# Whole-expert weight loads in the middle of a mixture-of-experts stream

## The reference, cut to what matters

```
h = rms_norm(x, moe_norm)
logits = h @ router_w + router_b                  # 32 experts, top 4 of each token
for each expert e, for its tokens xb:
    gu = xb @ w_up[e] + b_up[e]                   # w_up[e]: 1024 x 2048 float32 = 8 MB
    x_glu, x_lin = split(gu, 2)                   # clamped at 7
    act = x_glu * sigmoid(1.702 * x_glu) * (x_lin + 1)
    y = act @ w_down[e] + b_down[e]               # w_down[e]: 1024 x 1024 float32 = 4 MB
x = x + sum over the token's experts of gate * y
```

## Time and profile before

| | |
|---|---|
| median of the runs | 1144.08 us |
| the profiled execution | 1143.59 us, its span 1141.8 us |
| PE busy | 1100.4 us (96%) |
| DVE, ACT, POOL busy | 334.5, 231.0, 20.9 us |
| read from HBM | 446.18 MB, 392 GB/s over the span |
| DMA share, from slice 9 on to the last but one | 9 tenths or more |

### The profile page before, as it was taken

The page is one execution under the profiler, slowest core; times in us unless marked ns, Lnnn a source line. Parts: engine busy times, 40 slices in busy tenths (PEclk is TensorE's granted clock), DMA queues, the critical chain, the costliest instruction groups (busy, mean ns, idle before and its releaser), DMA issues.

```text
span 1141.8 us, 14032 instructions
## 1 busy us (share of the span) xinstructions
PE 1100.4 (96%) x5777; PEld 528.3 (46%) x5777; DVE 334.5 (29%) x641; ACT 231.0 (20%) x331; POOL 20.9 (2%) x34
## 2 busy tenths in 40 slices
PE   8999999999999999999999999999999999999997
PEld 8999998433333333333333333333333333333336
DVE  6899997311111111111111111111111111111027
ACT  6555454210011010110100010100100000011026
POOL 1200000000000000000000000000000000000011
PEclk9999999999999999999999999999999999999999
DMA  9985589899999999999999999999999999999991
GB/s 301 351 298 158 184 314 385 345 429 432 429 429 430 432 432 432 429 430 430 430 428 432 432 432 432 430 430 425 431 429 436 430 432 432 424 426 429 428 396 52
DMA packets 41055, 447.75 MB, mean 392 GB/s; under 512 B 3459, under 2 KB 3707, under 8 KB 21851
## 3 DMA queue, kind: packets, MB, share of 16 engines
q1 hardware_dynamic: 39924, 444.43, 93.4%
q0 software_dynamic: 672, 1.99, 0.6%
q10 hardware_dynamic: 423, 0.82, 0.2%
HBM read 446.18 MB, written 1.05 MB: 392 GB/s over the span
## 4 chain that ended last, share of the span: by engine, by line
PE 68%; DMA 28%; DVE 1%; ACT 1%; issue 1%; SPq 0%; DVEq 0%; ACTq 0%
PE ps L2080 24%; PE ps L2120 15%; DMA down_ring<-in_expert_w_down_dram 15%; DMA up_ring<-in_expert_w_up_dram 12%; PE ps L1797 6%; PE ps L2134 4%; PE ps L1807 3%; PE ps L1984 3%; PE ps L1861 2%; PE ps L2238 2%; PE ps L1887 1%; ACT hT L995 1%; PE ps L1866 1%; PE ps L2108 1%; PE ps L2091 1%; PE ps L2101 1%
## 5 line engine op out<-in xcount | busy, mean ns | idle before, releaser
L2080 PE MATMUL ps<-up_ring,hT 128*64 128x512 f32 x1968 | 432.7, 597 | 8.9 <-DMA up_ring<-in_expert_w_up_dram 8.4
L2080 PEld LDWEIGHTS ps<-up_ring,hT 128*64 128x64 f32 x1968 | 143.7, 138 | 289.1 <-issue 274.9
L2120 PE MATMUL ps<-down_ring,hT 128*64 128x512 f32 x992 | 229.3, 605 | 18.6 <-DMA down_ring<-in_expert_w_down_dram 11.9
L1535 DVE TENSOR_SCALAR extra<-ps 128x512 f32<-128x512 f32 x32 | 22.1, 692 | 690.4 <-PE ps L2091 690.4
L2120 PEld LDWEIGHTS ps<-down_ring,hT 128*64 128x64 f32 x992 | 68.2, 138 | 155.1 <-issue 139.4
L990 ACT ACTIVATE work<-ps 128x512 f32<-128x512 f32 x31 | 18.5, 597 | 437.7 <-PE ps L2091 437.7
L2134 PE MATMUL ps<-hT,extra 64*128 64x512 f32 x256 | 72.0, 640 | 0.8 <-DVE hT L1575 0.8
L1797 PE MATMUL ps<-h_hi,w_hi 128*128 128x256 f32 x288 | 70.2, 284 | 0.0
L1797 PE MATMUL ps<-h_lo,w_hi 128*128 128x256 f32 x288 | 69.9, 283 | 0.0
L802 ACT ACTIVATE w_hi<-up_ring 128x2048 fp32r<-128x2048 f32 x28 | 53.5, 1915 | 60.7 <-DMA up_ring<-in_w_in_dram 25.7
L492 DVE TENSOR_TENSOR w_lo<-up_ring,w_hi 128x2048 fp32r<-128x2048 f32 x28 | 63.9, 2288 | 4.1 <-ACT w_hi L802 4.0
(11 more groups left out here) (317 smaller groups left out, 818.6 us busy)
## 6 DMA issues: line engine op xcount, KB each, us to landing
up_ring<-in_expert_w_up_dram SPq DMA_DIRECT2D x47, 4096.0 KB, 27.4
down_ring<-in_expert_w_down_dram SPq DMA_DIRECT2D x63, 2048.0 KB, 18.3
up_ring<-in_expert_w_up_dram SPq DMA_DIRECT2D x31, 2048.0 KB, 17.5
up_ring<-in_w_in_dram SPq DMA_DIRECT2D x21, 1024.0 KB, 7.4
up_ring<-in_branch_w_dram SPq DMA_DIRECT2D x6, 1024.0 KB, 5.0
up_ring<-in_w_out_dram SPq DMA_DIRECT2D x4, 1024.0 KB, 6.9
up_ring<-in_expert_w_up_dram SPq DMA_DIRECT2D x4, 1024.0 KB, 22.6
up_ring<-in_ple_gate_w_dram SPq DMA_DIRECT2D x4, 1024.0 KB, 25.9
```

Source lines behind the costliest of these rows:

```text
L1535: nc.vector.tensor_scalar(lin, ps[:, LIN, :], 1.0 + LIMIT, 1.0 - LIMIT, ALU.min, ALU.max).then_inc(lin_ready, 1)
L2080: ins = nc.tensor.matmul(ps[64 * g:64 * g + 64, GLU + side, :], xe_of(q, j)[:, k % 4, k // 4, :], gated_columns(w, side, g), start=(k == 0 ...
L2120: last = nc.tensor.matmul(ps[64 * g:64 * g + 64, Y, :], actT[:, r, c, :], down_units[:, c, D * r + 512 * g:D * r + 512 * (g + 1)], start=( ...
```

## The change

- `EARLY_LOADS` goes from 16 to 20, so the order turns at 20 to 25.
- `JOINED_DOWN` (experts 4 to 19): both down units in one load of 4 MB (`load_down_pair`), issued when the expert before has read both; PE waits for it once, ahead of the first unit.
- `WHOLE_UP` (experts 6 to 19): all four up units in one load of 8 MB (`load_up_all`, 64 KB in one piece per partition), issued when expert q - 2 has read all four; PE waits for it once, ahead of the first unit.
- Rows by eights: partition p holds rows 8p to 8p + 7 of `w_up`, for all experts and all kinds of load. The gather (`x_eights`, `x_pairs`) and `moe_gain` follow.
- PE's and ACT's loops: four rounds of the projection with two pairs of experts each (projection before experts 4, 8, 12, 16), and then a loop of its own over experts 20 to 27, whose loads come in halves again.
- Ahead of PE's loops stand two new waits, on the semaphores of the third up unit of each buffer, since within the loop the second half is not waited for.

```
-EARLY_LOADS = 16
+EARLY_LOADS = 20
 JOINED_UP = range(4, N_EXP - 4)
+JOINED_DOWN = range(JOINED_UP.start, EARLY_LOADS)
+WHOLE_UP = range(JOINED_UP.start + 2, EARLY_LOADS)
...
+            def load_up_all(j, e):
+                first = UP_UNITS * j
+                rows = expert_w_up[0, bass.ds(e, 1)].rearrange("a (p r) n -> p a (r n)", p=P)
+                sp.dma_start(up_units[:, first:first + UP_UNITS, :].rearrange("p s b -> p (s b)"), rows[:, 0, :]
+                             ).then_inc(up_loaded[first], 16)
...
+            def load_down_pair(e):
+                rows = expert_w_down[0, bass.ds(e, 1)].rearrange("a (p r) n -> p a (r n)", p=P)
+                sp.dma_start(down_ring[:, :, :].rearrange("p s b -> p (s b)"), rows[:, 0, :]
+                             ).then_inc(down_loaded[0], 16)
...
+            def refill_up_all(q, j, e):
+                sp.wait_ge(up_used, UP_UNITS * (q - 1))
+                load_up_all(j, e)
...
+            def refill_down_pair(q, e):
+                sp.wait_ge(down_used, DOWN_UNITS * (q - 1) + DOWN_UNITS)
+                load_down_pair(e)
...
             refill_up_pairs(e + 1, 1, e + 1)
-            refill_down(e, e)
+            refill_down_pair(e, e)
             with sp.Fori(e // 2 + 1, EARLY_LOADS // 2) as i:
                 for j in range(2):
-                    refill_up_pairs(2 * i + j, j, 2 * i + j)
-                    refill_down(2 * i + j - 1, 2 * i + j - 1)
+                    refill_up_all(2 * i + j, j, 2 * i + j)
+                    refill_down_pair(2 * i + j - 1, 2 * i + j - 1)
...
-                                                x_sb[:, a, 512 * g:512 * (g + 1)], start=(a == 0), stop=(a == TT - 1))
+                                                x_eights[:, a, g, :, :], start=(a == 0), stop=(a == TT - 1))
...
-                    elif c % 2 == 0:
-                        pe.wait_ge(up_loaded[UP_UNITS * j + c], 16 * turn + 16)
+                    elif c == 0:
+                        pe.wait_ge(up_loaded[UP_UNITS * j], 16 * turn + 16)
+                    elif c == 2 and (halves or isinstance(q, int)):
+                        before = 0 if isinstance(q, int) and q < WHOLE_UP.start else len(WHOLE_UP) // 2
+                        pe.wait_ge(up_loaded[UP_UNITS * j + c], 16 * (turn - before) + 16)
...
             pe.wait_ge(early_unit_loaded, 16)
+            for j in range(2):
+                pe.wait_ge(up_loaded[UP_UNITS * j + 2], 16 * WHOLE_UP.start // 2)
             with pe.Fori(0, PROJ_PARTS) as part:
...
+            with pe.Fori(EARLY_LOADS // 2, JOINED_UP.stop // 2) as i:
+                for j in range(2):
+                    expert(2 * i + j, j, i, part=PROJ_PARTS - 1, halves=True)
```

More of the change, by code:

```diff
@@ L104 @@
 FINAL_BANK = [4, 5, 6, 7, 0]
-EARLY_LOADS = 16
+EARLY_LOADS = 20
 JOINED_UP = range(4, N_EXP - 4)
+JOINED_DOWN = range(JOINED_UP.start, EARLY_LOADS)
+WHOLE_UP = range(JOINED_UP.start + 2, EARLY_LOADS)
 PROJ_PARTS = 4
-PAIRS = len(JOINED_UP) // 2 // PROJ_PARTS
-assert JOINED_UP.start + 2 * PAIRS * PROJ_PARTS == JOINED_UP.stop
+PAIRS = len(JOINED_DOWN) // 2 // PROJ_PARTS
+assert JOINED_DOWN.start + 2 * PAIRS * PROJ_PARTS == JOINED_DOWN.stop
 CONV_UNIT = 5
@@ L543, in load_up @@
                 landed = up_loaded[UP_UNITS * j + c] if landed is None else landed
[L544 to L545 removed]
+                rows = expert_w_up[0, bass.ds(e, 1)].rearrange("a (p c r) n -> p (a c) (r n)", p=P, r=UP_ROWS)
+                sp.dma_start(up_units[:, UP_UNITS * j + c, :], rows[:, c, :]).then_inc(landed, 16)
             def load_up_pair(j, h, e):
                 first = UP_UNITS * j + 2 * h
[L549 removed]
+                rows = expert_w_up[0, bass.ds(e, 1)].rearrange("a (p h r) n -> p (a h) (r n)", p=P, r=2 * UP_ROWS)
                 sp.dma_start(up_units[:, first:first + 2, :].rearrange("p s b -> p (s b)"), rows[:, h, :]
+                             ).then_inc(up_loaded[first], 16)
[3 more added lines that the diff above has]
+                sp.dma_start(up_units[:, first:first + UP_UNITS, :].rearrange("p s b -> p (s b)"), rows[:, 0, :]
                              ).then_inc(up_loaded[first], 16)
@@ L586, in _ @@
             load_down(0, 0)
-            early_rows = expert_w_up[0, EARLY_EXPERT].rearrange("(h p r) n -> p h r n", p=P, r=2 * UP_ROWS)
+            early_rows = expert_w_up[0, EARLY_EXPERT].rearrange("(p h r) n -> p h r n", p=P, r=2 * UP_ROWS)
             sp.dma_start(early_rows_at[0], early_rows[:, 0, 0, :]).then_inc(single_rows_loaded, 16)
-            rows = expert_w_up[0, 0].rearrange("(h p r) n -> p h r n", p=P, r=2 * UP_ROWS)
+            rows = expert_w_up[0, 0].rearrange("(p h r) n -> p h r n", p=P, r=2 * UP_ROWS)
             for r in range(UP_ROWS):
@@ L617, in refill_down @@
                     load_down(c, e)
+            def refill_down_pair(q, e):
+                sp.wait_ge(down_used, DOWN_UNITS * (q - 1) + DOWN_UNITS)
+                load_down_pair(e)
             def load_last_rows(j, e):
                 c = UP_UNITS - 1
-                rows = expert_w_up[0, e].rearrange("(h p k r) n -> p h k r n", p=P, k=2, r=UP_ROWS)
+                rows = expert_w_up[0, e].rearrange("(p h k r) n -> p h k r n", p=P, k=2, r=UP_ROWS)
                 for r in range(UP_ROWS):
@@ L741, in _ @@
             pool.dma_start(rb[:, :], on_all(router_b[0])).then_inc(mats_loaded, 16)
-            pool.dma_start(moe_gain[:, :].rearrange("p (h r) -> p h r", h=2),
-                           moe_norm[0].rearrange("(h p r) -> p h r", h=2, p=P)).then_inc(mats_loaded, 16)
+            pool.dma_start(moe_gain[:, :], moe_norm[0].rearrange("(p r) -> p r", p=P)).then_inc(mats_loaded, 16)
             pool.wait_ge(mats_loaded, 64)
@@ L1026, in _ @@
                         expert(JOINED_UP.start + 2 * PAIRS * part + 2 * i + j)
+            with act.Fori(EARLY_LOADS // 2, JOINED_UP.stop // 2) as i:
+                for j in range(2):
+                    expert(2 * i + j)
             for q in range(AHEAD, N_EXP - 1):
@@ L2044, in single_loads, with up @@
                 return sum(e not in loads for e in range(q % step, q + 1, step))
-            def up(q, j, turn, first=False, last=False, early_result=False):
+            def up(q, j, turn, first=False, last=False, early_result=False, halves=False):
                 pe.wait_ge(xe_ready, 1 if first else gathered(q) + 2)
@@ L2109, in act_columns, with down_landed, down @@
                 last.then_inc(actT_done, 1)
-            def down(q, c, last=False):
+            def down_landed(q, c, halves=False):
+                if c == 0:
+                    pe.wait_ge(down_loaded[0], 16 * q + 16)
+                elif halves:
+                    pe.wait_ge(down_loaded[1], 16 * (q - len(JOINED_DOWN)) + 16)
+                elif isinstance(q, int):
+                    pe.wait_ge(down_loaded[1], 16 * sum(e not in JOINED_DOWN for e in range(q + 1)))
+            def down(q, c, last=False, halves=False):
                 pe.wait_ge(actT_ready, q + 1)
@@ L2116, in down @@
                     pe.wait_ge(last_half_loaded, 16)
-                pe.wait_ge(down_loaded[c], 16 * q + 16)
+                down_landed(q, c, halves)
                 for r in range(DOWN_ROWS):
@@ L2149, in ple_projection, with expert @@
                 last.then_inc(ple_proj_done, 1)
-            def expert(q, j, turn, first=False, part=None, last=False):
-                up(q, j, turn, first=first, last=last)
+            def expert(q, j, turn, first=False, part=None, last=False, halves=False):
+                up(q, j, turn, first=first, last=last, halves=halves)
                 if part is not None:
@@ L2165, in expert @@
                     picked_to_columns(q + 1)
-                down(q, 0, last=last)
+                down(q, 0, last=last, halves=halves)
                 if isinstance(q, int) and q == AHEAD:
@@ L2172, in expert @@
                     to_tokens(q - 1, 1)
-                down(q, 1, last=last)
+                down(q, 1, last=last, halves=halves)
                 if isinstance(q, int) and q == AHEAD + 1:
```

13 lines of the change are left out of this document (7 added, 6 removed).

## The result

The changed kernel takes 1155.01 us (median of five runs; the kernel before 1144.00 beside it): a ratio of 1.0098, with a 95% interval of 1.0087 to 1.0108. A sixth run, of 1260.41 us at a granted clock of 0.85, was in a slow state and is left out (the median of all six is 1155.37 us). The changed kernel is some 11 us slower. I had forecast 5.9 us slower, in a range of 2.5 to 7.9. The direction and the place were right, the size was half.

The account below looks back on a forecast made before the run. The prediction took the stream of loads, which has no hole, to bound the kernel. Restart, joins and code fetches summed to 7.9 - 2.3 + 0.3 = 5.9 us slower, 1150.0 us, with its own range 1147.5 to 1151.9.

Parts of the forecast that it names:

- What bounds the kernel: Whole kernel: bound by the stream of loads, 29.22 us an expert against PE's 26.88; any hole is paid in full.
- Rival 2: Behind the hole at expert 6: the DMA engines catch up, only the joins are left, -2.0 us, 1142.1 us; chance 7%.
- Part 1: 14 up loads (experts 6 to 19) and 15 down loads: each join saves 0.08 us, 2.3 us less in all.
- Part 2: Restart at expert 6: PE's new wait (4.6 us) and asking for the whole buffer (3.3) make the stream 7.9 us late.
- Rival 1: Waits ahead of PE's loops: already met, only the whole buffer's hole of 3.3 us counts, +1.3, 1145.4 us; chance 7%.
- Rival 3: Up loads: rows 64 KB apart in place of 32 KB slow them by 1%, 5.0 us more, 1155.0 us; chance 5%.
- Rival 4: Whole up loads: 64 KB pieces go as two of 32 KB, 14 savings of 0.08 us lost, 1151.1 us; chance 15%.
- Part 3: Experts 7 to 19, after the restart: no further hole, 2.3 us to spare at up(7), later least slack 2.7 us.
- Part 4: Experts 19 to 27: PE still waits at expert 27's second half, by some 1.6 us, so the stream's shift stays.
- Part 5: Small parts: gather, projection's places and ACT's loop cost nothing; fetching PE's extra loop code near expert 20 costs 0.3 us.

## Why the prediction was wrong in size

- **What bounds the kernel: right.** Every gap in the stream came back in the time, and behind the hole the period is 29.06 us, shorter than before by the gain of the joins alone. Rival 2 (caught up) is refuted.
- **Part 1, the joins: right.** 0.16 us per expert in the chain, 1.1 us for the 16 down joins by the medians.
- **Part 2, the restart at expert 6: the step that failed.** Its term was 7.9 us and measured 12.8. The issue of up(6) came 3.4 us later than I wrote (341.7 for 338.35): 0.9 us for a landing and a wake-up that came later, and 2.4 us for the halved clock, which the working left out although it had PE idle for 4.6 us. The rest, 1.6 us, is the load itself, 23.3 us to landing for the 21.7 that I took. Most of it lies on one DMA engine: the trace has sixteen completions for each load, which I take for one from each of the 16 DMA engines, and of those of up(6) fifteen stand from 362.9 to 363.6 us, the last at 365.1. In all six traces with a whole up(6) the last is 0.8 to 1.5 us behind the fifteenth. In each of the six an instruction fetch of 16 KB falls into the load (at 358.3 us in the changed kernel); that it is the cause isn't shown. Of the 8.7 us that the changed kernel takes over the version without the stop, 8.3 are the later landing of up(6), and 8.0 of these its later issue (341.7 for 333.7): the wait and the clock. My upper bound of 8.7 us for this term rested on the second load of rows 7, which I had called one into an idle queue; the load ahead of it landed at 217.8 us, 1.8 after its issue at 216.0.
- **Rival 1, the stop without effect: right as a price.** I gave 1145.4 us for the hole of the whole buffer alone; the version with exactly that took 1146.3. In its trace up(6) lands 4.5 us late, where this rival had 3.3.
- **Rival 3, the row pitch: refuted**, by the version with the layout alone (pieces up to 32 KB) and by those with whole up loads from 8 or 12 on (64 KB).
- **Rival 4, 64 KB pieces going as two: refuted** by the packets of the changed kernel from 380 to 480 us:

```profile
DMA packets 965, 42.86 MB, mean 429 GB/s; under 512 B 111, under 2 KB 111, under 8 KB 111
```

  Without the 111 small ones that is 50 KB a packet, which pieces of at most 32 KB can't give.
- **Part 3, "no further hole": wrong.** I had 2.7 us of slack at the least. Against down(12)'s landing at 578.2, up(14) was issued at 575.2, and a start takes 2.3: 0.7 us. What is missing is that PE, after waiting for down(11), fell to half clock again, 1.7 us in this row of the changed kernel (3.65 us is the usual for such 16 matmuls), ahead of the projection at expert 12:

```profile
549.20 5.35 PE L2159 MATMUL ps<-down_ring,hT 128*64 128x512 f32 x16 [2.48 <-DMA down_ring<-in_expert_w_down_dram]
```

  With 0.7 us left a hole still appeared. A landing is the last of sixteen completions, and down(12)'s stand from 576.1 to 578.2 us, so by a start of 2.3 us (577.5) fourteen of the sixteen engines had run out of work. That the middle one of up(14)'s completions is 0.9 us late and the last 1.9 is not explained. The same hole at up(10) in the second profile of the changed kernel bears the reading out; no run takes the projection or the half clock away by itself.
- **Part 4: right.** PE still waited at expert 27.
- **Part 5: nearly right.** Layout, gather and loops cost nothing (run by itself: 1143.99). What the fetched code costs was not tried apart. The late half of up(21) may be it: a fetch of 16 KB stands at 792.9 us, and of the load's sixteen completions only the last is late (795.0 us, where 9.7 behind the load ahead would be 793.3). That would be 1.7 us for my 0.3; other versions with the second loop show from nothing to 1.4 us there, so the cause stays open.

The sum as it was in the profiled execution, from the landings: 12.8 at expert 6, less 2.2 for the 28 joins behind it, plus 1.9 at up(14), plus 1.7 at up(21), less 1.0 at the end, where before a load of expert 31 was 1.1 us late on one engine (the wait of 0.54 us in rows 9) and now isn't. That gives 13.2 for the 13.1 us in the span. Of two profiles the small holes differ, so only the first term is one of the kernel; the others are of this execution. The medians of the two sets of runs are 1155.0 and 1154.1 us.

## What to carry to other kernels

When a stream of loads bounds a kernel, joining loads saves little (0.08 us a join here) and puts at stake much, because a larger load is issued only when its whole buffer is free. Ask for each wait ahead of an issue how much is still queued at that moment; if it is less than a start (2.3 us here) plus the jitter of the consumer and of the DMA engines, the larger load makes a hole that is never caught up. In the traces of this case ten 8 MB loads were issued with 3.0 to 3.2 us still queued, and seven of them landed 0.4 to 2.0 us late; of the 96 with 4.7 us or more queued one was late by more than 0.2 (0.8 us). Let a wait on a landing stand where the data is read and not ahead of a loop (8.7 us here), and price a stop of PE as its length plus the slow work behind it.

## What was not expected of the hardware

- PE's stops are dearer than they are long: after 5.23 us idle the granted clock was 0.50, and a projection of 1.99 us took 3.78. Shorter ones count too: after 2.48 us of waiting, 3.65 us of matmuls took 5.35.
- A load that is issued when the queue is all but empty costs 2.4 to 2.5 us over its data at 4 MB (12.1 and 12.2 us for 9.7), and 3.9 over 19.4 for 8 MB (23.3 us; 23.0 in the version without the stop), of which 1.2 to 1.5 us lie on the last of its sixteen completions alone. 8 MB loads issued with 4.7 us or more queued show no such excess.
- The first and the last of a load's sixteen completions stand apart, and stay so from load to load: some 2.5 us apart in the kernel before from 340 us on, 2.1 in the changed kernel up to up(14), 2.9 to 3.0 behind it and 4.4 behind up(21). The landing tells the slowest engine; the first runs dry that much sooner.
